# Where the weight sums of the last MLP chunk are formed, in a decoder trunk on one core

## The reference, cut to what matters

```python
D_MODEL, SEQ, DEPTH = 1024, 512, 2
D_FF = 4 * D_MODEL
...
    h2 = rmsnorm(x, g_ffn)
    x = x + jnp.square(jax.nn.relu(h2 @ w_up)) @ w_down
```

## Time and profile before

| | |
|---|---|
| median of 3 runs | 1923.71 us (1923.6 to 1926.04) |
| the profiled execution, its own time | 1923.79 us |
| span in its trace | 1922.0 us |
| PE busy | 1866.2 us, 97% of the span |
| DVE busy | 1255.4 us, 65% |
| ACT busy | 837.4 us, 44% |
| POOL busy | 134.2 us, 7% |
| mean granted PE clock | 0.988 of full speed |

### The profile page before, as it was taken

One profiled execution on the slowest core, in us unless ns is written; L12 is line 12 of the kernel. 1 busy time (PEld: TensorE's weight loads), 2 busy tenths in 40 slices (PEclk: granted clock), 3 DMA queues, 4 the chain that ended last, 5 costly groups with the idle time before them and its releaser, 6 DMA issues.

```text
span 1922.0 us, 22976 instructions
## 1 busy us (share of the span) xinstructions
PE 1866.2 (97%) x9064; PEld 1551.0 (81%) x9064; DVE 1255.4 (65%) x1848; ACT 837.4 (44%) x1234; POOL 134.2 (7%) x108
## 2 busy tenths in 40 slices
PE   9999999999999999999599999999999999999995
PEld 7888888887888888888488888888878888888874
DVE  5356878867557576677563658778664565676765
ACT  7325465464223344443372265565632334433434
POOL 0001201200000000001000112111000000010010
PEclk9999999999999999999799999999999999999997
DMA  4543324324333555468426333233243335555683
GB/s 146 208 147 113 102 67 124 102 67 143 99 99 116 127 150 134 135 150 241 87 82 242 102 95 112 68 113 115 65 152 100 99 110 131 133 131 151 157 219 88
DMA packets 213547, 241.12 MB, mean 125 GB/s; under 512 B 13632, under 2 KB 160832, under 8 KB 212672
## 3 DMA queue, kind: packets, MB, share of 16 engines
q1 hardware_dynamic: 193712, 201.03, 33.0%
q0 software_dynamic: 19008, 37.75, 11.4%
q10 hardware_dynamic: 720, 0.87, 0.1%
HBM read 225.86 MB, written 13.77 MB: 125 GB/s over the span
## 4 chain that ended last, share of the span: by engine, by line
PE 87%; DMA 5%; DVE 3%; ACT 2%; issue 2%; POOL 0%; SPq 0%; ACTq 0%; DVEq 0%; POOLq 0%
PE pj L1851 19%; PE pj L1853 19%; PE pj L1852 19%; DMA u<-in_w_down 2%; PE sc L2157 1%; PE sc L2159 1%; PE sc L2161 1%; PE yr L2157 1%; PE yr L2159 1%; PE yr L2161 1%; DMA gh<-in_w_down 1%; PE pt L2161 1%; PE pt L2159 1%; PE pt L2157 1%; DVE w_lo L1176 1%
## 5 line engine op out<-in xcount | busy, mean ns | idle before, releaser
L1851 PE MATMUL pj<-h_hi,w_hi 128*128 128x512 f32 x1408 | 554.4, 394 | 1.1 <-DVE sA L1551 1.1
L1853 PE MATMUL pj<-h_hi,w_lo 128*128 128x512 f32 x1408 | 548.5, 390 | 0.0
L1852 PE MATMUL pj<-h_lo,w_hi 128*128 128x512 f32 x1408 | 548.3, 389 | 0.0
L1176 DVE TENSOR_TENSOR w_lo<-w_raw,w_hi 128x1024 fp32r<-128x1024 f32 x283 | 334.9, 1220 | 120.6 <-ACT w_hi L703 119.3
L703 ACT CAST w_hi<-w_raw 128x1024 fp32r<-128x1024 f32 x280 | 282.9, 1050 | 280.3 <-PE pj L1853 56.9
L1851 PEld LDWEIGHTS pj<-h_hi,w_hi 128*128 128x128 f32 x1408 | 264.3, 188 | 59.2 <-DVE sA L1551 2.0
L1853 PEld LDWEIGHTS pj<-h_hi,w_lo 128*128 128x128 f32 x1408 | 264.3, 188 | 55.8
L1852 PEld LDWEIGHTS pj<-h_lo,w_hi 128*128 128x128 f32 x1408 | 264.5, 188 | 54.1 <-issue 0.5
L718 ACT CAST w_hi<-gh 128x1024 fp32r<-128x1024 f32 x84 | 83.9, 1049 | 133.4 <-DMA gh<-in_w_down 72.3
L1128 POOL TENSOR_TENSOR rcos<-rot,tables 128x512 f32<-128x512 f32 x64 | 87.2, 1363 | 711.7 <-ACT rot L829 652.7
L1176 DVE TENSOR_TENSOR w_lo<-gh,w_hi 128x1024 fp32r<-128x1024 f32 x84 | 99.0, 1221 | 48.0 <-ACT w_hi L718 47.7
(11 more groups left out here) (340 smaller groups left out, 3161.0 us busy)
## 6 DMA issues: line engine op xcount, KB each, us to landing
w_raw<-in_w_in SPq DMA_DIRECT2D x151, 512.0 KB, 4.7
w_raw<-in_w_up SPq DMA_DIRECT2D x64, 512.0 KB, 4.8
gh<-in_w_down POOLq DMA_DIRECT2D x28, 1024.0 KB, 8.5
gh<-in_w_down SPq DMA_DIRECT2D x16, 1024.0 KB, 5.9
w_raw<-in_w_down SPq DMA_DIRECT2D x20, 512.0 KB, 5.0
w_raw<-in_w_b SPq DMA_DIRECT2D x16, 512.0 KB, 3.5
w_raw<-in_w_o SPq DMA_DIRECT2D x16, 512.0 KB, 4.0
u<-in_w_down POOLq DMA_DIRECT2D x8, 1024.0 KB, 12.3
```

Of the source, the lines that this page charges most:

```text
L1176: nc.vector.tensor_tensor(w_lo[s][:, c], src[:, c], w_hi[s][:, c], ALU.subtract).then_inc(lo_done, 1)
L1851: nc.tensor.matmul(out, w_hi[s][:, wc], acts[0], start=first, stop=False)
L1852: nc.tensor.matmul(out, w_hi[s][:, wc], acts[1], start=False, stop=False)
L1853: return nc.tensor.matmul(out, w_lo[s][:, wc], acts[0], start=False, stop=last)
```

## The change

In the last chunk of each layer, `spares[4]` no longer starts from B11. The place becomes `spares[6]` and `spares[4]` at once. SP waits until `gh` holds B11+B12 and copies it into the place (SBUF to SBUF), POOL adds B22 there for D3.6, and, when D3.6's weights have been split, POOL adds B21 in the same place for D3.4. `gh` gets no second add. `spares[7]` is formed as before, but its load is now issued behind the copy, where before it was ahead of the load for `spares[4]`. POOL's adds in the last chunk are 4 where they were 6; SP issues as many transfers as before, one of them now a copy. ACT and DVE take D3.6's weights from the spare place instead of `gh`.

```diff
@@ adds_of
-        return (2 if as_sum else 0) if c == CH - 1 else (3 if as_sum else 1)
+        return (1 if as_sum else 0) if c == CH - 1 else (3 if as_sum else 1)
@@ the places
-        spares = {7: spare[:, 0:4, :].rearrange("p k c -> p (k c)"), 4: spare[:, 4:8, :].rearrange("p k c -> p (k c)")}
+        spare_parts = [spare[:, 4 * i:4 * i + 4, :].rearrange("p k c -> p (k c)") for i in range(2)]
+        spares = {6: spare_parts[0], 4: spare_parts[0], 7: spare_parts[1]}
@@ SP
                         sp.wait_ge(a_ready, l * LD + d_no(c, 4) + 1)
-                        for i, src in ((7, w_down_q[l, c + 1, 1, 1]), (4, w_down_q[l, c + 1, 0, 0])):
-                            sp.dma_start(spares[i].rearrange("p (k c) -> p k c", k=4), src).then_inc(spare_in[i], 16)
+                        slot = slot_of(l, c + 1, True)
+                        sp.wait_ge(sum_added[slot], (adds_before(l, c + 1, True) + 1) * 16)
+                        sp.dma_start(spares[6], gh[slot][:]).then_inc(spare_in[0], 16)
+                        sp.dma_start(spares[7].rearrange("p (k c) -> p k c", k=4),
+                                     w_down_q[l, c + 1, 1, 1]).then_inc(spare_in[1], 16)
@@ ACT, hi_sum
-                if c == CH - 1 and i in (7, 4):
-                    act.wait_ge(spare_added[i], (l + 1) * 16 * {7: 1, 4: 3}[i])
+                if c == CH - 1 and i in spares:
+                    act.wait_ge(spare_added[i == 7], {6: 2 * l + 1, 4: 2 * l + 2, 7: l + 1}[i] * 16)
@@ POOL
-                def add_spare(i, n, h, m):
-                    if n == 0:
-                        pool.wait_ge(spare_in[i], l * 16 + 16)
+                def add_spare(i, h, m):
+                    if i == 4:
+                        pool.wait_ge(lo_done, m_unit(l, "D", CH - 1, 6) * 2 + 2 + UNIT_CREDIT)
                     else:
-                        pool.wait_ge(spare_added[i], (l * 3 + n) * 16)
+                        pool.wait_ge(spare_in[i == 7], l * 16 + 16)
                     nc.gpsimd.dma_start(spares[i].rearrange("p (k c) -> p k c", k=4), w_down_q[l, CH - 1, h, m],
-                                        accum_op=ALU.add).then_inc(spare_added[i], 16)
+                                        accum_op=ALU.add).then_inc(spare_added[i == 7], 16)
...
                 add_quarter(CH - 1, 1, True, 0, 1)
-                add_spare(4, 0, 0, 1)
-                add_spare(7, 0, 0, 1)
-                add_spare(4, 1, 1, 1)
-                add_spare(4, 2, 1, 0)
-                add_quarter(CH - 1, 5, True, 1, 1)
+                add_spare(6, 1, 1)
+                add_spare(7, 0, 1)
+                add_spare(4, 1, 0)
```

More of the change, by code:

```diff
@@ L405, in trunk @@
         sum_added = [sem(f"sum_added{i}") for i in range(2)]
-        spare_in = {i: sem(f"spare_in{i}") for i in (7, 4)}
-        spare_added = {i: sem(f"spare_added{i}") for i in (7, 4)}
+        spare_in = [sem(f"spare_in{i}") for i in range(2)]
+        spare_added = [sem(f"spare_added{i}") for i in range(2)]
         a_sum = sem("a_sum")
@@ L1626, in weights_low @@
                             for hf in range(2):
-                                lo_half(n, n % 2, hf, spares[i] if c == CH - 1 and i in (7, 4) else
+                                lo_half(n, n % 2, hf, spares[i] if c == CH - 1 and i in spares else
                                         gh[slot_of(l, c, i in (1, 5, 6, 4))])
```

## The result

The changed kernel takes 1880.98 us (median of 4 runs, 1880.63 to 1883.43) beside 1924.59 us for the one before: 43.6 us less. The ratio is 0.9776, 95% interval 0.9759 to 0.9793, which is 40 to 46 us. The forecast was 1876.4, the range 1874.4 to 1883.0. The stall is gone, but a small wait is left in each layer, and with it 4.3 us are lost that the forecast had counted as won.

A forecast was written before the change was run, and what follows sets the result against it. PE, busy 97% of the span, bounds the kernel; its stalls at D3.6 cost 24.76 and 22.63 us, so 1923.79 - 47.39 = 1876.4 us, all other steps costing 0. The range was 1874.4 to 1883.

The forecast's parts named there:

- The stall and its price: PE waits for D3.6's weights behind POOL's queue order; 24.76 us lost in layer 0, 22.63 in layer 1, together 47.39.
- Steps 1 to 3: Last chunk: SP's new wait costs 0, the copy lands in 7.3 us at 891, POOL's add of B22 lands 903.7.
- Step 6, the tightest link: POOL's last add, B21 for D3.4, lands at 920 to 924.2, needed by 926.5; cost 0, slack 2.3 us at worst.
- a small wait is left: Rival, 11%: earlier adds delay raw of D3.2, or D3.4's sum is late; 2 to 3.3 us per layer, 1880.4 to 1883.
- the slack of 3.8 us given to raw: Layer 1, D3.2's second half: w_lo at about 1863.6, PE wants it at 1867.4, so 3 us of delay are covered.
- step 4: DVE's result of D3.5 starts at 907.81; w_lo halves for D3.6 ready by 910.2 and 911.3; DVE keeps up.
- a slow copy: Rival, 4%: the copy takes 20 us, D3.6's sum is 6.1 us over per layer; 1888.6 and some 4 more at worst.
- a copy on few engines: Rival, 3%: one DMA engine or few carry the copy, which takes 41 us; slower, 1926 to 1934, say 1930.
- no change: Rival, 2%: the stall was not POOL's order, D3.6 waited on something else and the wait stays; 1923.7.

The follow-up runs named there:

- the add behind D3.2: Changed kernel, but POOL's add for D3.6 also waits until D3.2's weights are split (about 906): 1890.70 us.
- the pair in the order of before: Changed kernel with SP's two issues swapped back, the load for D3.7 first and the copy for D3.6 second: 1876.71 us.
- the reordered kernel before: The kernel before, with POOL's add for D3.6 into gh moved ahead of the second and third add into the spare place; all six adds stay: 1896.29 us.
- the DVE sum moved: Changed kernel with DVE's activation sum for D3.3 moved behind w_lo for D3.6, in the D3.2 step: 1887.79 us.

## Why the prediction was right, and where it failed

**The stall and its price: right.** The prediction named POOL's queue and priced the loss start to start, at 47.39 us. The five kernels of the experiments with a loss of at most 0.11 us come out where that says: 1876.36 to 1876.93, against 1876.4.

**Steps 1 to 3: right.** SP had no wait for `gh`. The copy landed after 6.8 us (7.3 was taken from the load it replaces), and the first add, issued at 890.43, took 13.6 us (12.7 taken) to 904.0 (903.7 forecast). The 2.45 us from ACT's start to PE's start came again in both layers of the run with the add behind D3.2.

**Step 6, the tightest link: right.** The last add took 8.4 us from 915.52, and PE did not wait for it.

**What failed** is the choice between the forecast, at 80%, and the rival "a small wait is left", at 11%, which is what came: 1880.98, in its 1880.4 to 1883. It named the cause as it was: adds up to 3 us earlier, raw for D3.2 late. The measured time is inside the stated range only because the range reached to this rival. The step that failed is the slack of 3.8 us given to raw. It was reckoned against the moment when PE wants that half. Raw came 3.8 to 4.2 us later than before, at the edge of that slack, and PE indeed hardly waited there, but step 4 had DVE start D3.5's result at 907.81 as before; behind the late half it starts at 911.54. The slack of raw for DVE's queue is what counts, and it was about 2.2 us: with raw's second half 1.67 us ahead of D3.2's start, in place of 3.88, the loss is 0.11 (the pair in the order of before), and with 0.36 us behind it PE waits 1.60. DVE doesn't make the delay good in the step that follows: its four instructions there take 5.68 us from start to start (911.54 to 917.22), where a unit on PE takes 5.44, and D3.3 comes another 0.23 us late. The loss of 2.15 is 1.92 at D3.6 and this.

The rival's time was in part luck. It took 2 us of cost from a delay of 6 us against a slack of 3.8; the delay was 3.8 to 4.2, for which that slack gives 0 to 0.4 us per layer. The cost of 2.15 and 2.17 came another way, through DVE's queue.

**The rule of the Trainium skill** that this rival leaned on (DMA: Bandwidth & Descriptors, section Queues, rings and completion order: engines go round the queues that have work) agrees with the runs in direction: adds started later, in an otherwise equal kernel, give raw in time. The delay, 3.8 to 4.2 us, was more than the 3 that the prediction worked out from it, and the runs can't tell taking turns from another way of sharing. By the Trainium skill's other rule cited (the same page, section Why a DMA increments its semaphore by 16 and not by 1) the copy gets all 16 engines. Its 6.8 us agree: one sixteenth of 407 GB/s would need 41.

**The other rivals:** a slow copy, a copy on few engines and no change did not occur.

## What to carry to other kernels

When a queue's order brings late-needed work ahead of early-needed work, price the stall from start to start, with the slow matmuls behind it. Then ask of every transfer that will now start earlier what it meets; here two lines of SP, in the other order, are worth as much as a tenth of the whole change. A slack is to be reckoned through the instructions queued behind the late one on its engine, not only to the user of the late data: here 2.2 us in place of 3.8. And before moving an instruction back, list who reads its result.

## What the runs showed of the hardware

- A gap of 2.0 us in PE's starts (changed kernel) left the clock at full speed (granted 1.00 from 912 to 916 us), with a pitch of 0.23 us soon behind it. Behind one of 6.4 us (the add behind D3.2, layer 0) 12 steps from start to start were 0.43 us, at a granted clock of 0.50, and behind one of 5.4 us (the reordered kernel before, layer 1) 11. Behind one of 4.6 us (the add behind D3.2, layer 1) there were 8, beginning 1.3 us after PE was back. Of the 9.0 us lost behind D3.2 in the case of 6.4 us, 5.99 are the wait, and the other 3.0 are almost all the longer steps.
- With the DVE sum moved, a gap of only 2.72 us in layer 0, after one of 0.87 and one of 0.46, was followed by 8 steps of 0.43 us, beginning about 1 us after PE was back (granted 0.50 from 923 to 925 us). In layer 1 of the same execution a gap of 2.75 us, after one of 0.84 and one of 0.68, was followed by none (granted 1.00 from 1861 to 1866). PE in the two layers, about 2 us behind the gap:

```profile
923.15 0.63 PE L2161 MATMUL pt<-w_hi,a_hi 128*128 128x512 f32 x1
...
1863.13 0.40 PE L2161 MATMUL pt<-w_hi,a_hi 128*128 128x512 f32 x1
```

- So the gap alone does not say whether the clock falls; nor do the small gaps just ahead of it, which were much the same in both layers.
- A 1 MB accumulating transfer landed 8.4 us after its issue when alone, 13.6 as the first of two in flight and 17.7 as the second (changed kernel, layer 0). With the pair in the order of before, the second one took 20.4. One from SBUF to SBUF took 6.8 and 7.1 us, a load of that size in its place 7.8 and 7.4.
